# A one-core encoder layer with 32 experts: the sum of the expert outputs is kept in the output tensor, in place of a DRAM array of its own that is copied at the end

## What is computed

```python
    x = x + jnp.concatenate([a, r], axis=-1) @ w_out[l]          # "the mix": (1024, 1024)
    h2 = rms_norm(x, norm2_g[l])
    x = x + moe_ffn(h2, ...)

def moe_ffn(h, ...):
    top_val, top_idx = lax.top_k(h @ w_router + b_router, 4)      # 4 of 32 experts per token
    gate = softmax(top_val)
    # for each expert, on the rows of the tokens that chose it:
    gu = xblk @ w_gate_up[e] + b_gate_up[e]
    act = g_lin * sigmoid(1.702 * g_lin) * (u_lin + 1.0)          # clipped halves of gu
    yb = act @ w_down[e] + b_down[e]
    y = zeros.at[row_tok].add(yb * row_g[:, None])                # rows are added up per token
```

## Time and profile before

| | |
|---|---|
| median of three runs | 2073.35 us (2070.44, 2073.35, 2073.68) |
| span of the profiled execution | 2064.5 us |
| TensorE busy in the span | 1899.4 us, 92% |
| VectorE, ScalarE, GpSimd busy | 75%, 69%, 29% |
| moved by DMA | 479.28 MB, mean 232 GB/s |

### The profile page before, as it was taken

One profiled execution on the slowest core, in us unless ns is written; L12 is line 12 of the kernel. 1 busy time (PEld: TensorE's weight loads), 2 busy tenths in 40 slices (PEclk: granted clock), 3 DMA queues, 4 the chain that ended last, 5 costly groups with the idle time before them and its releaser, 6 DMA issues.

```text
span 2064.5 us, 61180 instructions
## 1 busy us (share of the span) xinstructions
PE 1899.4 (92%) x25003; PEld 1587.8 (77%) x25003; DVE 1550.4 (75%) x2115; ACT 1422.4 (69%) x1851; POOL 592.4 (29%) x448
## 2 busy tenths in 40 slices
PE   5999998889979869999999999999999899899896
PEld 3444883333554469999999999999999899899896
DVE  5331332788572268888999899999989999999896
ACT  4331332777563458887788888888878888888884
POOL 3222121667651232112221232122223213213221
PEclk8999999999899969999999999999999999999998
DMA  5111100000133358899999999999999999999996
GB/s 173 41 41 62 42 22 1 1 1 1 32 131 128 139 199 316 301 322 323 318 339 330 343 330 340 327 341 343 352 338 339 351 340 348 348 341 349 352 313 230
DMA packets 142379, 479.28 MB, mean 232 GB/s; under 512 B 15140, under 2 KB 30244, under 8 KB 142240
## 3 DMA queue, kind: packets, MB, share of 16 engines
q1 hardware_dynamic: 129440, 444.13, 59.7%
q0 software_dynamic: 12864, 34.09, 6.9%
HBM read 457.34 MB, written 34.87 MB: 238 GB/s over the span
## 4 chain that ended last, share of the span: by engine, by line
PE 30%; DVE 13%; issue 11%; DMA 6%; ACT 4%; DVEq 1%; POOL 0%; POOLq 0%; SPq 0%; ACTq 0%
PE banks L1779 27%; DVE region_c L1057 8%; DMA region_a<-w_down_dram 5%; DVE region_b L1604 2%; ACT region_b L1449 1%; ACT region_b L1453 1%; DVE region_b L1609 1%; PE banks L1745 1%; PE banks L1772 1%; DVE region_b L1624 1%; ACT region_b L1437 1%; DVE region_b L1619 1%; DMA region_b<-rows_out,region_d 1%; ACT region_b L1439 1%; DVE region_b L1615 0%
## 5 line engine op out<-in xcount | busy, mean ns | idle before, releaser
L1779 PE MATMUL banks<-region_b,region_c 128*128 128x128 f16 (+2 forms) x18432 | 1142.3, 225 | 60.3 <-DVE region_b L1624 32.2
L1779 PEld LDWEIGHTS banks<-region_b,region_c 128*128 128x128 f16 x18432 | 1125.1, 98 | 67.8 <-ACT region_b L1453 34.1
L1057 DVE TENSOR_TENSOR region_c<-region_a,region_c 128x2048 f16<-128x2048 f32 x256 | 574.2, 2284 | 3.9 <-DMA region_b<-rows_h,region_d 3.9
L1052 ACT ACTIVATE region_c<-region_a 128x2048 f16<-128x2048 f32 x256 | 478.4, 1910 | 46.0 <-DMA region_a<-w_down_dram 20.3
L1378 POOL TENSOR_TENSOR region_d<-region_d 80x1 f32<-80x1 f32 x96 | 60.6, 631 | 930.8 <-DVE region_d L1577 624.8
L1057 DVE TENSOR_TENSOR region_c<-region_d,region_c 128x2048 f16<-128x2048 f32 x128 | 287.0, 2283 | 0.0
L1052 ACT ACTIVATE region_c<-region_d 128x2048 f16<-128x2048 f32 x128 | 238.0, 1918 | 0.7 <-DMA region_d<-w_gate_up_dram 0.7
L353 PE MATMUL banks<-region_a,region_d 128*128 128x512 f16 x960 | 209.7, 381 | 1.7 <-PEq L96 1.7
L353 PEld LDWEIGHTS banks<-region_a,region_d 128*128 128x128 f16 x960 | 94.1, 98 | 117.5 <-issue 6.5
L1461 ACT ACTIVATE region_b<-banks,region_d 80x512 f32<-80x512 f32 x128 | 80.5, 677 | 140.2 <-PE banks L1772 140.2
L1367 POOL DMA_INDIRECT region_b<-rows_h,region_d x64 | 135.8, 2122 | 44.2 <-issue 44.2
(11 more groups left out here) (301 smaller groups left out, 2168.9 us busy)
## 6 DMA issues: line engine op xcount, KB each, us to landing
region_d<-w_gate_up_dram SPq DMA_DIRECT2D x128, 1024.0 KB, 8.6
region_a<-w_gate_up_dram SPq DMA_DIRECT2D x128, 1024.0 KB, 8.1
region_a<-w_down_dram SPq DMA_DIRECT2D x128, 1024.0 KB, 8.4
region_d<-w_in_dram SPq DMA_DIRECT2D x14, 1024.0 KB, 4.9
region_b<-x_dram SPq DMA_DIRECT2D x4, 1024.0 KB, 9.6
region_b<-w_out_dram SPq DMA_DIRECT2D x8, 512.0 KB, 3.5
rows_out<-region_b SPq DMA_DIRECT2D x8, 512.0 KB, 2.6
rows_h<-region_b SPq DMA_DIRECT2D x8, 512.0 KB, 2.7
```

Source lines behind the costliest of these rows:

```text
L1052: act.activation(part_hi[r][:, 2 * q:2 * q + 2, :], raw[r][:, 2 * q:2 * q + 2, :], ACT.Copy).then_inc(s_hi9, 1)
L1057: dve.tensor_tensor(part_lo[r][:, at, :], raw[r][:, at, :], part_hi[r][:, at, :], ALU.subtract).then_inc(s_lod, 1)
L1779: mm = pe.matmul(out_ap, a, b, start=(first and s == 0), stop=(k == KT - 1 and s == 2), skip_group_check=True)
```

## The change

`rows_out` is now a name for the output tensor itself: the mix is stored into `out`, the items' rows are added onto `out`, the last item's rows are read from `out` and written into `out`. The four copies on SP, the semaphore `out_stored` and the waits on it are gone. In their place POOL waits for its own two reads of the last rows before it writes.

```diff
-        rows_out = nc.dram_tensor("rows_out", (T, D), F32, kind="Internal").ap()
+        rows_out = out[0]
...
                 item_loads(n_last, True)
-                sp.wait_ge(s_scat, n_items * 32 + CSC)
-                for q in range(4):
-                    sp.dma_start(out[0, q * (T // 4):(q + 1) * (T // 4), :], rows_out[q * (T // 4):(q + 1) * (T // 4), :]).then_inc(s_out, 16)
-                sp.wait_ge(s_out, 64)
                 sp.wait_ge(s_fin, 32)
...
-                pool.wait_ge(s_out, 64)
+                pool.wait_ge(s_ybase, 32)
                 for h in range(2):
                     pool.wait_ge(s_yadd, 2 * h + 2)
-                    pool.indirect_dma_start(out=out[0], out_offset=bass.IndirectOffsetOnAxis(ap=rows_prev[:, h:h + 1], axis=0),
+                    pool.indirect_dma_start(out=rows_out[:, :], out_offset=bass.IndirectOffsetOnAxis(ap=rows_prev[:, h:h + 1], axis=0),
                                             in_=yrow[:, h, :], in_offset=None, bounds_check=T - 1, oob_is_err=False).then_inc(s_fin, 16)
```

More of the change, by code:

```diff
@@ L1276, in build_trunk @@
         s_xg, s_xgT, s_xhi, s_xlo = sem("x_gathered"), sem("xg_turned"), sem("x_hi_ready"), sem("x_lo_ready")
-        s_yT, s_yrow, s_scat, s_init, s_out, s_id = sem("y_turned"), sem("y_scaled"), sem("y_added"), sem("init9"), sem("out_stored"), sem("ident16_ready")
+        s_yT, s_yrow, s_scat, s_init, s_id = sem("y_turned"), sem("y_scaled"), sem("y_added"), sem("init9"), sem("ident16_ready")
         y_base = region_b[0:HS, 8192 + 6 * D:8192 + 8 * D].rearrange("p (h d) -> p h d", h=2)
```

## The result

The changed kernel took 0.9957 of the time of the kernel before, 95% interval 0.9941 to 0.9972, over 19 runs of each: 0.43% faster, or 8.9 us of 2065.86. The medians are 2059.46 us (2053.46 to 2068.43) and 2065.86 us (2060.78 to 2074.14). Taken by themselves they are 6.4 us or 0.31% apart, which is inside the interval as well, so the size of the gain is known only as some 6 to 12 us. The forecast was 7.3 us or 0.35%, also inside, but its time of 2066.1 us and its range from 2062.0 us up both lie above the 2059.46 us measured. The level it started from, 2073.35 us, was the median of three runs that stand high among the 19.

The account below looks back on a forecast made before the run. It took matmuls and weight loads to bound the items, and the wait for POOL's second read the end. Gains of 6.65 + 0.64 = 7.3 us from 2073.35 gave 2066.1 us, range 2062 to 2071.3 us.

Parts of the forecast that it names:

- What bounds: Items bound by matmuls and weight loads; at the end the core waits for POOL's second read of the last rows, 11.12 us.
- (a): Four copies on SP go: issuing and waiting worth nothing, only their DMA load under the two reads goes.
- (b): POOL's two reads of the last rows without the copy: second lands in 4.1 us instead of 11.1, at 2049.2.
- (c): At the end, TensorE's transposes are late next: VectorE's first group starts at 2049.66 instead of 2056.31, gain 6.65 us.
- (d): TensorE's second pass over the last rows runs at full clock instead of half, gain 0.64 us.
- (e): Tail behind VectorE's end: last write issued 0.85 us later, lands after 3.2 us, span ends about 0.6 us later; all stays.
- (f): POOL's new wait for its own two reads before the last writes: costs nothing and gives nothing.
- (g): Stores, additions and reads in the output tensor: same count, shape and queues, only the address differs; taken as nothing.
- Rival 1: Last rows' reads slow by themselves, 9.0 us: 2071.2 us, no measurable change; chance 0.13.
- second form: Copy costs the last reads one queue turn of 3.0 us: 2070.3 us, within 0.2%; counted in the 0.13.
- Rival 2: Items' additions onto the output tensor take longer: slower, 2165 us at twice the present 7.3 us each; chance 0.04.
- Rival 3: Items' weight loads disturbed by the move, up to 6 us: about 2072 us, no change; chance 0.08 with anything like it.

Follow-up runs that it names:

- e6: Kernel before with 56 extra TensorE transposes between its two passes over the last rows; from VectorE's first group to the span's end 7.8 us (before 8.2).
- e2: Changed kernel with four 1 MB copies put back, into a scratch array nobody uses; ratio to before 1.0005, second read landed in 13.9 us.
- e3: Kernel before, copy started only after both reads of the last rows landed; 25.3 us from second read's issue to span's end (before 19.4).
- e4: Kernel before, copy in 4 KB pieces instead of 64 KB; 20.0 us from second read's issue to span's end (before 19.4).
- e8: Kernel before, copy started only once VectorE had set the last rows' numbers; 22.1 us from second read's issue to span's end (before 19.4).
- e1: Kernel before with its own rows_out kept but the four copies and the wait on them left out; ratio to before 0.9978.
- e5: Kernel before with two of the four copies; 13.6 us from second read's issue to span's end (before 19.4).

## Why the prediction was right about the end and wrong about the time

**What bounds, (a) and (b): right.** The reads' 11 us were the copy's. Without it they take 4.0 to 4.2 us (4.1 forecast from the first two gathers), with a stand-in copy 13.9 us, with half a copy 5.4 us.

**(c), TensorE's turning comes last: right, 0.1 us off.** VectorE starts 0.78 us behind the first pass; the forecast had 0.68 us (2049.66 - 2048.98). It follows TensorE's fourth transpose by 0.13 us (2058.82 - 2058.69), not by the 0.05 us taken from the second pass.

**(d), the clock: right.** VectorE's four groups take 2.88 us, the forecast's 1.48 + 1.40. e6 shows the same 0.64 us between first and last group with the copy in place. In the end of the span some 0.4 us of it arrives there.

**(e), the tail: right to 0.15 us.** The last write is issued 0.85 us behind VectorE's end (2062.55 - 2061.70), as before; from its issue to the end of the span it is 4.0 us where it was 3.8. e6, which keeps the copy but not the slow second pass, has 4.0 us as well (2062.8 - 2058.77), so it goes with the writes, which are then issued 1.4 us apart and not 2.1. With the 0.1 us of (c) this is the difference between 7.3 and the 7.0 us of the profiles.

**(f) and (g), the new wait and the output tensor: right as far as it can be seen.** The additions land in 7.7 us in the median (7.6 before), and in the two pairs of runs the changed kernel has ratios of 0.9957 and 0.9954, the kernel with its own array 0.9978 and 0.9946.

**The rivals.** Rival 1, reads slow by themselves, falls with 4.1 us. Its second form, one turn of some 3 us, falls too: the delay grows with what is left of the copy, from 1.4 us (5.4 - 4.0) to 9.9 us (13.9 - 4.0). That the size of the pieces matters is true (5.3 us between 64 KB and 4 KB), only the price is not one piece. Rival 2 did not come about: the additions land in 7.7 us. Rival 3 at its 6 us would have left no change. The intervals of both sets of runs of the changed kernel end at 0.9972, 5.8 us below before, and the end alone gave 7.0 us, so some 1 us is what the items can have lost by this reckoning; none of it is shown.

**The step that failed** is the last of the sum: "The median of the runs lies 8.9 us above that span; I leave that as it is". The profile's span and the runs' times came from different executions, and three runs were taken as the level. In all 19 runs of the changed kernel the time is 1.7 to 1.9 us above the span of the same run (2068.37 and 2066.5 us for the profiled one), and in the 57 further runs of the kernel before, beside the experiments, it is so too. By that the profiled execution of before took about 2064.5 + 1.8 = 2066.3 us, which is the median of the 19 runs, 2065.86, within half a microsecond; the three runs, 2070.44 to 2073.68, are all among the highest seven of the 19. From 2066.3 the sum of the forecast gives 2059.0, and the measured median is 2059.46. That the one profiled execution lies so near the median is luck, since single executions of this kernel lie over 13 us apart. The low end of the range fell with it, since its 4 us were taken from the spread of the same three runs, where larger sets of runs of that kernel are 13 to 19 us apart. With the row for the span at hand, the level should have been bounded by both, the span from below and the runs from above.

**What stays open.** The ratio gives 8.9 us (5.8 to 12.2), the medians 6.4 us and the profiles' ends 7.0 us; these agree within the interval, and no gain beyond the end is shown. But the 7.0 us rest on one profiled execution of the kernel before, and kernels with a copy do not always end alike. In four of the twelve profiles (e2, e3, e4 and e8, all with a copy) the last addition landed only 2.5 to 2.6 us ahead of the second read, and VectorE's next step waited for it, where it landed 5.4 to 6.7 us ahead in the others. In e2 and e8 the copy then stood closer to the reads and the end took 22.9 and 20.8 us. How often the kernel before runs so, and why just these four did, was not tried.

## What to carry to other kernels

A DMA that nobody on the path waits for still holds up those that are waited for: ask of each bulk copy which small indirect read is issued behind it, and, where the copy has large pieces as here (64 KB), expect the read to land with the end of the copy. Take such a gain from the stage's own rows, from a point that both kernels share, and take the level from more than one execution: here the 7 us are about half of what separates the fastest and the slowest run of the same kernel. When a wait goes, look at the clock of the engine that stood still in it; it gives back a little more.

## What the runs showed of the hardware that was not expected

POOL's issue of one and the same indirect addition took 1.42 us or 6.93 us. Rows of the profile of before and of e2, at the same place of the program:

```profile
2027.45 1.42 POOL L1372 DMA_INDIRECT rows_out<-region_b,region_d  x1 [0.89 <-issue]
2027.72 4.48 DVE L1057 TENSOR_TENSOR region_c<-region_a,region_c 128x2048 f16<-128x2048 f32 x2
```

```profile
2022.23 4.48 DVE L1058 TENSOR_TENSOR region_c<-region_a,region_c 128x2048 f16<-128x2048 f32 x2
2022.36 6.93 POOL L1373 DMA_INDIRECT out_dram<-region_b,region_d  x1 [1.29 <-issue]
2026.63 1.35 DVE L1610 TENSOR_TENSOR region_b<-region_b 128x384 f32<-128x384 f32 x3
2028.77 0.29 DVE L1616 TENSOR_SCALAR region_b<-region_b 128x256 f32<-128x256 f32 x1 [0.70 <-ACT region_b L1450]
```

Where POOL began 0.27 us ahead of VectorE's pair of long subtractions it was done in 1.42 us; where it began 0.13 us behind them it ended at 2029.29, after VectorE's next pause (from 2028.07 to 2028.77). This is the same start as that of the late additions above. The Trainium skill ("DMA: Bandwidth & Descriptors", SWDGE vs HWDGE vs iDMA) says that GpSimd writes the descriptors of its DMAs into SBUF state that VectorE locks it out of during its two-port modes. No row here shows whether these subtractions run in such a mode, and no run took them away, so this stays a guess. In e3, e4 and e8 POOL also began just behind such a pair (0.02 to 0.41 us) and took 6.6 to 7.0 us. One profile speaks against a plain lock: in e1 POOL began 0.63 us behind the pair (2035.51 and 2034.88) and was done after 2.95 us, at 2038.46, while VectorE was in it until 2039.37:

```profile
2034.88 4.49 DVE L1057 TENSOR_TENSOR region_c<-region_a,region_c 128x2048 f16<-128x2048 f32 x2 [0.16 <-ACT region_c L1052]
2035.51 2.95 POOL L1368 DMA_INDIRECT rows_out<-region_b,region_d  x1 [2.03 <-issue]
```

TensorE's clock fell after a shorter stand than the profile of before suggested. In e5 the engine stood still from 2050.80 to 2052.18; the windows:

```profile
2050.80:2052.10 1.30, 0.00 (x1) 0.00 (x0) 0.73 (x2) 0.00 (x0) 0.00 (x0) 0.95 0.00 0
2052.10:2054.20 2.10, 1.93 (x8) 1.35 (x8) 1.48 (x4) 0.00 (x0) 0.51 (x1) 0.50 0.00 0
```

Its second pass ran at 0.50 and took 1.93 us, after 1.4 us of standing still, while in the changed kernel the clock stayed at 1.00 over 0.5 us. In e3 it stood still for 2.4 us:

```profile
2047.30:2049.70 2.40, 0.00 (x0) 0.00 (x1) 0.80 (x2) 0.00 (x0) 0.00 (x0) 1.00 0.12 50
2049.70:2050.50 0.80, 0.80 (x5) 0.52 (x6) 0.69 (x2) 0.00 (x0) 0.00 (x0) 0.79 2.73 900
```

The clock was 1.00 over all of it and 0.79 in the mean of the next 0.8 us, in which the pass had begun. So a wait of 1.4 us was enough to lose the full clock once, and one of 2.4 us was not enough another time.
